# The delta rule's inverse of all eight heads in common visits, and its recurrence in step

## The reference

```python
lmat = where(strict, einsum('bhnid,bhnjd->bhnij', k_beta, k) * decay, 0)
t_inv = triangular_solve(eye + lmat, eye)      # lower, unit diagonal, 64 x 64
u = t_inv @ v_beta
w = t_inv @ (k_beta * exp(g_cum))
attn_intra = where(lower_incl, einsum('bhnid,bhnjd->bhnij', q, k) * decay, 0)
def step(state, xs):                            # four chunks, one after another
    u_c, w_c, qd_c, a_c, kt_c, cd_c = xs
    v_new = u_c - w_c @ state
    o = qd_c @ state + a_c @ v_new
    return state * cd_c + swapaxes(kt_c) @ v_new, o
```

## Time and profile before

| | |
|---|---|
| median of three runs | 2109.33 us (2109.28 to 2109.83) |
| the profiled execution, device time | 2108.79 us |
| its span from the first to the last instruction | 2107.0 us |
| TensorE busy with matmuls | 2087.3 us |
| VectorE busy | 1617.6 us |
| ScalarE busy | 1321.4 us |

### The profile page before, as it was taken

One profiled execution on the slowest core, in us unless ns is written; L12 is line 12 of the kernel. 1 busy time (PEld: TensorE's weight loads), 2 busy tenths in 40 slices (PEclk: granted clock), 3 DMA queues, 4 the chain that ended last, 5 costly groups with the idle time before them and its releaser, 6 DMA issues.

```text
span 2107.0 us, 35194 instructions
## 1 busy us (share of the span) xinstructions
PE 2087.3 (99%) x13756; PEld 1822.7 (87%) x13756; DVE 1617.6 (77%) x2935; ACT 1321.4 (63%) x2610; POOL 22.0 (1%) x42
## 2 busy tenths in 40 slices
PE   9999999999999999999999999999999999999998
PEld 9888888888888888888888888888888888988887
DVE  7899766787788888656888867777686777689874
ACT  7866457775676666544666666555566655567764
POOL 0000000000000000000000000000000000100000
PEclk9999999999999999999999999999999999999999
DMA  7544534665465565556656666555555565744564
GB/s 288 178 141 147 170 113 149 234 208 189 159 200 191 195 194 192 198 191 192 198 191 192 197 191 195 190 193 190 193 185 177 172 197 190 214 159 160 161 210 140
DMA packets 107813, 390.95 MB, mean 186 GB/s; under 512 B 12368, under 2 KB 12368, under 8 KB 106880
## 3 DMA queue, kind: packets, MB, share of 16 engines
q1 hardware_dynamic: 104896, 377.40, 55.0%
q0 software_dynamic: 2608, 11.04, 1.5%
q10 hardware_dynamic: 144, 0.26, 0.0%
HBM read 384.37 MB, written 2.13 MB: 183 GB/s over the span
## 4 chain that ended last, share of the span: by engine, by line
PE 89%; DVE 7%; ACT 3%; issue 1%; DVEq 0%; ACTq 0%
PE main L597 84%; PE two L597 4%; DVE W L1104 2%; ACT PPw L1824 1%; PE two L600 1%; ACT W L1824 1%; DVE gt L1104 1%; DVE GV L1110 0%; DVE PPw L1104 0%; ACT L1823 0%; DVE AQ L1104 0%; DVE GK L1110 0%; DVE PB L1104 0%; DVE RW L1726 0%; DVE GQ L1110 0%
## 5 line engine op out<-in xcount | busy, mean ns | idle before, releaser
L597 PE MATMUL main<-A,W 128*128 128x256 f32 (+2 forms) x7200 | 1248.0, 333 | 6.3 <-DVE W L1104 6.0
L1824 ACT ACTIVATE W<-RAW 128x512 fp32r<-128x512 f32 (+1 forms) x1400 | 866.4, 627 | 585.6 <-PE main L597 581.5
L597 PEld LDWEIGHTS main<-A,W 128*128 128x128 f32 (+1 forms) x7200 | 1087.6, 188 | 159.3 <-DVE W L1104 8.3
L1104 DVE TENSOR_TENSOR W<-RAW,W 128x512 fp32r<-128x512 f32 (+1 forms) x1400 | 945.1, 685 | 350.8 <-ACT W L1824 342.1
L597 PE MATMUL main<-H,W 128*128 128x512 f32 (+1 forms) x1408 | 239.7, 333 | 0.0
L597 PEld LDWEIGHTS main<-H,W 128*128 128x128 f32 x1408 | 212.1, 188 | 27.5
L597 PE MATMUL main<-B,W 128*128 128x512 f32 (+1 forms) x1216 | 197.0, 324 | 0.3 <-DVE B L1104 0.3
L597 PEld LDWEIGHTS main<-B,W 128*128 128x128 f32 x1216 | 176.4, 188 | 20.5 <-issue 0.5
L597 PE MATMUL main<-W,A 128*128 128x512 f32 (+1 forms) x672 | 150.2, 378 | 0.0
L597 PEld LDWEIGHTS main<-W,A 128*128 128x128 f32 x672 | 117.9, 188 | 22.4 <-issue 0.5
L597 PE MATMUL main<-W,B 128*128 128x512 f32 x384 | 88.2, 390 | 0.0
(11 more groups left out here) (331 smaller groups left out, 1382.2 us busy)
## 6 DMA issues: line engine op xcount, KB each, us to landing
RAW<-ws SPq DMA_DIRECT2D x700, 512.0 KB, 3.5
CB<-cscr POOLq DMA_DIRECT2D x4, 1024.0 KB, 5.0
HB<-head SPq DMA_DIRECT2D x7, 384.0 KB, 6.4
HB<-head SPq DMA_DIRECT2D x2, 1152.0 KB, 12.9
XT<-xT POOLq DMA_DIRECT2D x4, 512.0 KB, 7.3
MS<-memT POOLq DMA_DIRECT2D x4, 512.0 KB, 8.4
out<-YT SPq DMA_DIRECT2D x7, 256.0 KB, 2.6
CST<-cst SPq DMA_DIRECT2D x1, 1272.0 KB, 16.7
```

Of the source, the lines that this page charges most:

```text
L597: return e.matmul(o, l, r, start=start, stop=True, skip_group_check=True)
L1104: return e.tensor_tensor(o, a, b, op)
L1824: return e.activation(o, i, f, bias=bias, scale=scale, accum_out=accum)
```

## The change

- The levels leave `octet(g)` for a task of their own, `levels`, which begins at tick 127. Each of its visits does one product of one level for both groups, in two PSUM pairs. In a visit every quarter gets group 0's matmul and then group 1's.
- T times beta v and the product for w are done for both groups in one visit each.
- The short transposes go. VectorE transposes the whole t4 at once, and ScalarE copies the odd blocks across the halves to `t3x`.
- The clamps are done by ScalarE with Relu (of t0 and of -t0).
- ScalarE copies GV of the second group.
- Both groups' recurrence begins together at tick 155, in four steps instead of five. Its first step waits for all of WT.
- The output and the stick-breaking heads move by some ticks; a head's task has 11 ticks in place of 13.
- Tiles of both groups exist at the same time, so places are new and the counts on the semaphores change.

```diff
-T_RECUR = [149, 155]
-T_GOUT = {(0, 0): (160, 181), (1, 0): (166, 182), (0, 1): (172, 183), (1, 1): (178, 184)}
-T_SB = [172, 198]
+T_LEVELS = T_OCTET[1] + 17
+T_RECUR = [155, 155]
+T_GOUT = {(0, 0): (166, 181), (1, 0): (169, 182), (0, 1): (178, 183), (1, 1): (180, 184)}
+T_SB = [177, 199]
...
-        t0, t1, t2, t3, t4 = (at(f"gt{i}", 64 + 2 * i, [8, 64])[:] for i in range(5))
-        t5, t6 = at("gt5", 53, [2, 4, 128])[:], at("gt6", 74, [2, 4, 128])[:]
-        t7 = at("gt7", 128, [2, 4, 128])[:]
-        t6h, t6l = at("gt6h", 74, [2, 4, 128], R)[:], at("gt6l", 128, [2, 4, 128], R)[:]
+        inv = [[at(f"gt{g}{i}", kb, [8, 64])[:] for i, kb in enumerate(x)]
+               for g, x in enumerate(((64, 66, 68, 70, 72), (0, 2, 4, 6, 60)))]
+        t3x = [at(f"gt{g}3x", 58 + g, [4, 64])[:] for g in range(2)]
+        t5 = [at(f"gt{g}5", kb, [2, 4, 128])[:] for g, kb in enumerate((53, 48))]
+        t6 = [at(f"gt{g}6", kb, [2, 4, 128])[:] for g, kb in enumerate((74, 138))]
+        t7 = [at(f"gt{g}7", kb, [2, 4, 128])[:] for g, kb in enumerate((128, 134))]
+        t6h, t6l = at("gt6h", 138, [2, 4, 128], R)[:], at("gt6l", 134, [2, 4, 128], R)[:]
...
-        Q_PE, Q_VE, Q_AC, Q_MU = 20, 29, 11, 8
+        Q_PE, Q_VE, Q_AC, Q_MU = 7, 15, 4, 4
...
+            def levels():
+                rows, quarters = (slice(0, 64), slice(64, 128)), ((0, 0), (1, 1), (0, 1), (1, 0))
+                pre_ve, pre_ac, pre_mu = 2 * Q_VE, 2 * Q_AC, 2 * Q_MU
                 for lev in range(1, 6):
-                    w.wait_ge(qd_mu, mu + (2 if lev == 1 else 3 + lev))
-                    w.wait_ge(qd_ve, ve + 15 + 2 * lev)
-                    first(t2, t4)
+                    w.wait_ge(qd_mu, Q_MU + 2 if lev == 1 else pre_mu + 2 * lev - 2)
+                    w.wait_ge(qd_ve, pre_ve if lev == 1 else pre_ve + 4 * lev - 6)
+                    for m in range(4):
+                        for c, s in quarters:
+                            f = c ^ s
+                            for g in range(2):
+                                t2, t4 = inv[g][2], inv[g][4]
+                                z = mm(twos[g][rows[s], f, 64 * m:64 * m + 64], t2[rows[c], 2 * m + f, :], t4[rows[c], 2 * m + f, :])
+                    z.then_inc(qd_pe, 1)
                     yield from ticks(2)
-                    w.wait_ge(qd_ac, ac + 4 + lev)
-                    w.wait_ge(qd_ve, ve + 16 + 2 * lev)
-                    second(t3, t0)
+                    w.wait_ge(qd_ac, pre_ac + 4 * lev)
+                    w.wait_ge(qd_ve, pre_ve + 4 * lev - 4)
+                    for m in range(4):
+                        for c, s in quarters:
+                            f = c ^ s
+                            for g in range(2):
+                                t0, t3 = inv[g][0], inv[g][3]
+                                T = t3x[g][rows[s], m, :] if f else t3[rows[s], 2 * m, :]
+                                z = mm(twos[g][rows[c], f, 64 * m:64 * m + 64], T, t0[rows[s], 4 * f + m, :])
+                    z.then_inc(qd_pe, 1)
                     yield from ticks(3)
-                w.wait_ge(qd_ve, ve + 27)
-                for b, o in enumerate((X, Z)):
-                    for n in range(4):
-                        for P in rows:
-                            z = mm(o[P, 128 * n:128 * n + 128], t4[P, 4 * b + n, :], t5[P, b, n, :])
+                w.wait_ge(qd_ve, pre_ve + 18)
+                for g in range(2):
+                    for b in range(2):
+                        for n in range(4):
+                            for P in rows:
+                                z = mm(twos[g][P, b, 128 * n:128 * n + 128], inv[g][4][P, 4 * b + n, :], t5[g][P, b, n, :])
+                        z.then_inc(qd_pe, 1)
+                yield from ticks(3)
+                w.wait_ge(qd_ve, pre_ve + 20)
+                w.wait_ge(qd_ac, pre_ac + 22)
+                for g in (1, 0):
+                    for n in range(8):
+                        for c, P in enumerate(rows):
+                            z = mm(twos[g][:, c, 64 * n:64 * n + 64], t6[g][P, n // 4, n % 4, :], inv[g][4][P, n, :])
                     z.then_inc(qd_pe, 1)
-                yield from ticks(2)
-                w.wait_ge(qd_ve, ve + 29)
-                for n in range(8):
-                    for o, P in zip((X, Z), rows):
-                        z = mm(o[:, 64 * n:64 * n + 64], t6[P, n // 4, n % 4, :], t4[P, n, :])
-                z.then_inc(qd_pe, 1)
...
-                for step in range(5):
-                    now = [(g, step - g, half(step - g)) for g in range(2) if 0 <= step - g < 4]
+                for step in range(4):
+                    now = [(g, step, half(step)) for g in range(2)]
                     for g, c, P in now:
                         if c == 0:
                             w.wait_ge(l2_rs, 8)
-                            w.wait_ge(qd_ve, Q_VE * (g + 1))
-                            w.wait_ge(qd_ac, Q_AC * (g + 1))
+                            w.wait_ge(qd_ve, 2 * Q_VE + 20)
+                            w.wait_ge(qd_ac, 2 * Q_AC + 26)
                         if c:
                             w.wait_ge(rc_st[g], c)
                         w.wait_ge(rc_ac[g], c // 2)
...
-                w.wait_ge(qd_ve, ve + 3)
-                ts(t1, t0, 0.0, ALU.max).then_inc(qd_ve, 1)
-                ts(t2, t0, 0.0, ALU.min).then_inc(qd_ve, 1)
                 yield from ticks(4)
...
-                w.wait_ge(qd_ve, ve + 17)
-                cross().then_inc(qd_ve, 1)
                 for b in range(2):
                     q = GQ[:, h4, 128 * b:128 * b + 128]
-                    tt(q, q, t7[:, b], ALU.mult).then_inc(qd_mu, 1)
+                    tt(q, q, t7[g][:, b], ALU.mult).then_inc(qd_mu, 1)
+            def levels():
+                pre = 2 * Q_PE
+                yield
                 for lev in range(1, 6):
+                    if lev < 5:
+                        w.wait_ge(qd_pe, pre + 2 * lev - 1)
+                        for g in range(2):
+                            tt(inv[g][2], inv[g][1], bm(K[f"lm{lev + 1}"], 8), ALU.mult).then_inc(qd_mu, 1)
+                    yield from ticks(2)
+                    w.wait_ge(qd_pe, pre + 2 * lev)
+                    for g in range(2):
+                        by_half = inv[g][4].rearrange("p (m s) j -> p s m j", s=2)
+                        tt(by_half, by_half, twos[g][:, :, 0:256].rearrange("p s (m j) -> p s m j", m=4), ALU.subtract).then_inc(qd_ve, 1)
+                    if lev < 5:
+                        for g in range(2):
+                            w.wait_ge(qd_ve, 2 * Q_VE + 4 * lev - 3 + g)
+                            e.transpose(inv[g][3], inv[g][4]).then_inc(qd_ve, 1)
                     yield from ticks(3)
-                    if lev < 5:
-                        w.wait_ge(qd_pe, pe + 6 + 2 * lev)
-                        tt(t2, t1, bm(K[f"lm{lev + 1}"], 8), ALU.mult).then_inc(qd_mu, 1)
-                    yield from ticks(2)
-                    w.wait_ge(qd_pe, pe + 7 + 2 * lev)
-                    by_half = t4.rearrange("p (m s) j -> p s m j", s=2)
-                    tt(by_half, by_half, two[:, :, 0:256].rearrange("p s (m j) -> p s m j", m=4), ALU.subtract).then_inc(qd_ve, 1)
-                    if lev < 5:
-                        w.wait_ge(qd_ve, ve + 17 + 2 * lev)
-                        e.transpose(t3[:, 0::2, :], t4[:, 0::2, :])
-                        cross().then_inc(qd_ve, 1)
-                yield from ticks(3)
-                for b, o in enumerate((X, Z)):
-                    w.wait_ge(qd_pe, pe + 18 + b)
-                    e.tensor_copy(GV[:, h4, 128 * b:128 * b + 128], four(o[:])).then_inc(qd_ve, 1)
+                yield
+                for b in range(2):
+                    w.wait_ge(qd_pe, pre + 11 + b)
+                    e.tensor_copy(GV[:, 0:4, 128 * b:128 * b + 128], four(twos[0][:, b, :])).then_inc(qd_ve, 1)
...
-                w.wait_ge(qd_ve, ve + 5)
+                act(t1, t0, ACTF.Relu)
+                z = act(t2, t0, ACTF.Relu, scale=-1.0)
+                w.wait_ge(a_own, own(z))
                 act(t1, t1, ACTF.Exp, scale=-1.0).then_inc(qd_ac, 1)
-                act(t2, t2, ACTF.Exp).then_inc(qd_ac, 1)
-                yield from ticks(6)
+                act(t2, t2, ACTF.Exp, scale=-1.0).then_inc(qd_ac, 1)
+            def levels():
                 for lev in range(1, 6):
-                    yield from ticks(5)
-                    w.wait_ge(qd_pe, pe + 6 + 2 * lev)
-                    copy(halfs(fl(t0)), twos[0][:, :, 0:256]).then_inc(qd_ac, 1)
-                yield from ticks(7)
-                w.wait_ge(qd_pe, pe + 20)
-                for c, o in enumerate((X, Z)):
-                    to = WT[:, h4, :].rearrange("p h (b c j) -> p c b h j", b=2, c=2)[:, c]
-                    copy(to, o[:].rearrange("p (b h j) -> p b h j", b=2, h=4), scale=-1.0).then_inc(qd_ac, 1)
+                    w.wait_ge(qd_ve, 2 * Q_VE + 4 * lev - 4)
```

(33 more changed lines are left out.)

45 lines of the change are left out of this document (22 added, 23 removed).

## The result

The changed kernel takes 2117.36 us (median of 6 runs, 2116.36 to 2118.63); the kernel before, beside it, 2109.68 (2109.28 to 2110.07). The ratio is 1.0038, 95% interval 1.0028 to 1.0048. A second set gave 2117.24 against 2109.30, ratio 1.0037 (1.0025 to 1.0050). So it is slower by about 8 us. I had forecast 2108.6 us with a range up to 2114: wrong by 8.8 us, and on the side that I had given a chance of 0.2.

The account below looks back on a forecast made before the run. TensorE's own stream was taken as the bound, its matmuls busy 2087.3 of 2107.0 us. 2108.8 - 3.7 + 3.2 + 1.3 - 1.5 = 2108.1, on the median's scale 2108.6 us, range 2105 to 2114.

Parts of the forecast that it names:

- the side that I had given a chance of 0.2: Whole kernel: slower by more than 0.2%, chance 0.20; within 0.70, faster 0.10.
- levels: TensorE's level visits: 20 at 0.84 us become 10 at 1.31 us, -3.7 us.
- products and recurrence: Products behind the levels get shorter, recurrence longer as all 32 records fall on one half: +3.2 us together.
- new wait for WT: Recurrence step 0: TensorE waits for ScalarE's WT copies right behind the products, +1.3 us, once.
- waits that go, 133 to 188 us: TensorE's waits for level results and GV go, NTL waits stay or grow by tenths: -1.5 us, ends 0 and -2.4.
- heads: Stick-breaking heads, 5 ticks later and 2 ticks shorter each, stay hidden: nothing, or up to +2 us.
- if one fewer record fitted: Level visits: quarters would start 0.058 us apart, 0.17 us a visit, +1.7 us in all.
- the clamps: Two clamps moved from VectorE to ScalarE: worth nothing, or +0.5 us per group if the cover is thinner.
- rival 2: Levels: ScalarE's copies end last and each level waits, 5 us and more, 2114 to 2118; chance 0.12.
- rival 1: Level visits: the quarters lose their overlap, 3.3 us a visit, +20 us, 2129; chance 0.06.
- Rivals 3 and 4: Saturated stretch relaxes fully, WT copies hide: 2104 us, chance 0.08; halves still overlap in recurrence: 2103, chance 0.02.

Follow-up runs that it names:

- staggering alone: Changed kernel with the second group's recurrence again one step (6 half-chunks) behind the first's, in five steps: 2113.28 us.
- the filled wait: Changed kernel with 12 needless 128x512 matmuls put in front of TensorE's wait for the second group's gate products: 2115.17 us.
- five small edits: Changed kernel with gates' products early, level matmuls group by group, WT wait at first use, staggered recurrence, second group's heads at 13 half-chunks: 2101.61 us.
- levels group by group: Changed kernel with all 16 matmuls of group 0 ahead of group 1's in each level visit: 2115.22 us.

## Why the prediction was wrong

The sum had four terms, and two things had no term. In the profiled execution:

| | forecast | measured |
|---|---|---|
| levels | -3.7 | -2.2 (1.24 us a visit, not 1.09) |
| products and recurrence | +3.2 | not measured as a whole; fresh visit 3.99, as forecast; staggering alone gives 4.0 back |
| new wait for WT | +1.3 | +1.2 |
| waits that go, 133 to 188 us | -1.5 | +1.1 (idle 2.6 to 3.7) |
| clock behind an idle time | none | +3.0 (6.1 - 3.1; 2.7 against the filled wait) |
| heads | 0 | +2.1 in heads, +0.3 for GQ ahead of them |

With 3.2 taken for the second, this makes 8.7 us. Measured are 8.1 from the 400th main matmul, where the changed kernel is 0.6 us ahead, to the 1800th, where it is 7.5 behind; whole against whole the two profiled executions differ by 7.7.

1. **"Waits that go: -1.5, with 0 and -2.4 as ends" is the step that failed.** I had the direction of the utilisation right: VectorE near full, TensorE arriving sooner. From that I drew that NTL would grow by tenths. I did not ask what else TensorE would then arrive too early for. The first thing behind the first group's old levels that only VectorE can give it is the four gate products, 2.4 us in one piece at the end of VectorE's queue. In the kernel before they were ready (the last at 191.70) 0.6 us ahead of their use:

```profile
192.32 0.40 PE L597 MATMUL two<-gt6h,ONE 128*128 128x512 f32 x1
...
189.21 0.68 DVE L1104 TENSOR_TENSOR gt6h<-CST,ggh 128x512 fp32r<-128x512 f32 x1
```

   TensorE now wants them at 176.4, 15.9 us earlier (I had counted 12.7 us of visits, and 1.5 to 2.4 of waits beside them). VectorE begins them at 176.94, only 12.3 us earlier: by my count it lost 13.6 us of work, but it stood idle, waiting for ScalarE, where TensorE did not need it (0.61 us at 155 and 1.90 at 161 us). 15.9 - 12.3 - 0.6 = 3.0 us is the wait, but for 0.1. Up to there VectorE was busy for 39.09 of 43.40 us, 90%, where I had 97%:

```profile
133.00:176.40 43.40, 42.85 (x248) 37.44 (x246) 39.09 (x71) 37.17 (x66) 0.00 (x0) 1.00 0.57 185
```

   So VectorE even had more room than I gave it, and the wait came all the same: a mean over a stretch says nothing of who is late at its last microsecond. Making the gates' products early removed the wait; the range of the term did not hold its value and had no end above 0.
2. **The clock had no term.** The earlier trace rows showed PEclk 1.00, and I took full speed for given. The filled wait separates the two: idle time +3.1, clock +2.7 to 3.0 in the profiled execution and about half of it in most others. The Trainium skill ("TensorE: Matmul & The Clock Gate", Part 1, What's actually happening) says that the throttled clock is the default and activity releases it; the trace agrees (0.62 from 177 to 186 us behind the idle time, 1.00 with the same time filled). A term for it belonged beside each new wait of some microseconds. For WT's wait it was missing as well: of the nine executions profiled with that wait, the clock fell behind it in five.
3. **Levels.** I had named the bound myself: if one fewer record fitted, 0.17 us a visit, +1.7. It is 0.15 and +1.5. That the quarters run at once was right, and the value taken was the wrong end; the mixed visit of the earlier trace rows, from which I read it, has GK records of 128 columns on half the array, and did not tell how quarters start together.
4. **Heads: "Nothing, or up to +2".** I took 0; it is 2.1 us. I counted the slack of a link against its own chain and not against what stands ahead of it in VectorE's queue: at 393 us a B and a split of W, in order. At the old length of the links the waits are gone.
5. Right were the recurrence (3.99 a fresh visit), WT's wait, the clamps, that no copy of ScalarE's ends last in the levels (rival 2), and that the quarters keep their overlap (rival 1). Rivals 3 and 4 did not come either: no case of mine had the saturated stretch getting worse. The sign of the whole followed from the two terms that I had left at their friendly end and the two that I did not have.

What stays open: how long the low clock lasts behind one and the same wait. The granted clock from 177 to 186 us was 0.62 in two executions and 0.81 in the six others with that wait, of nearly the same program up to there.

## What to carry to other kernels

When you take work off an engine that is full beside another one, don't ask for the mean of the stretch but follow the earlier engine to the first result that it then wants, and look where that stands in the full engine's queue. Put a price on the clock behind each new idle time of TensorE of a microsecond or more, not on the idle time alone, and ask whether TensorE waits for something soon after: a later wait can take the price back. And where a change brings gain and loss in different places, move the losses one by one: here the same common levels ended 8 us above the kernel before with their surroundings as they stood and 7.5 below with five small edits.

## What the runs showed of the hardware

The granted clock fell behind the 3.1 to 3.2 us of idle time in all eight executions profiled with it, and in none of the three, nor in the kernel before, where it was gone or filled. Behind the 1.2 us wait for WT it fell in five of nine, and in none of the three where that wait was gone or had never been. The 1.8 us wait for NTL at 131 us is in all twelve profiles and the clock fell behind it in one (levels group by group):

```profile
131.00:133.00 2.00, 0.16 (x2) 0.08 (x1) 2.00 (x5) 1.99 (x4) 0.00 (x0) 1.00 0.18 55
133.00:138.00 5.00, 5.00 (x19) 4.31 (x20) 4.67 (x8) 3.24 (x5) 0.00 (x0) 0.66 0.54 190
```

PEclk is 0.66 there, and from the 700th to the 750th main matmul this execution takes 12.7 us, where that of the changed kernel takes 11.0 with the same program. So a short wait has a price that differs from execution to execution, and single profiles of two kernels can differ by 1 to 2 us at a place where their programs are the same.

Nor does every low stretch cost something. All twelve profiles, the kernel before's too, have a 2.1 us wait for W that ends between 1907 and 1925 us, where the program is that of the kernel before. Behind it the clock fell in seven, the changed kernel's among them. In the five others TensorE then waits 1.2 to 1.3 us for W a second time, about 37 us later; in the seven it does not, because it comes later. The changed kernel is 7.6 us behind at the 10000th main matmul, 9.0 at the 10400th and 7.7 at the 10800th. Its only wait from 1900 to 1960 us, and the clock:

```profile
PE main L601 <- DVE W L1109: 2.1, 1, 2.1
...
1922.00:1927.00 5.00, 4.51 (x17) 3.89 (x18) 4.79 (x13) 2.13 (x10) 0.00 (x0) 0.66 0.45 134
```

The mean granted clock of a whole execution, which is on record for every run, was 0.997 to 1.000 for the kernel before and 0.996 to 0.998 for the changed one. So one profile of the kernel before without such a fall does not mean that it never has one.

The order in which small matmuls go to the quarters of the array matters: with two float32 records in a row for each quarter a visit of 64 took 1.09 us, with four 1.24. Halves of the array run beside each other (1.99 us for 32 records of 128 columns) and records of one half one after another (3.77).
